# Combining expert results: second row added by an accumulating transfer instead of TensorE, residual rows and norm loaded into freed weight slots

## The chip, the cores and the metric

One Trainium2 chip (trn2), one core. The metric is the device time of one execution in microseconds (us); where several runs are told, it is their median.

## The reference

The model is a block of two layers on 1040 rows (16 meta rows and 1024 tokens) of width 1024, all in float32. Each layer is a mixer, a layer norm, a mixture of experts and a second layer norm; layer 0's mixer is an S5 scan beside differential attention, layer 1's is an RG-LRU. Every row goes to two of 32 experts, and the diff concerns what happens to their results:

```python
for i in range(DEPTH):
    ...
    h = _layer_norm(ALPHA * h + mix, *norms[i][0]).astype(dt)
    h = _layer_norm(ALPHA * h + _hier_moe(h, *moes[i]), *norms[i][1]).astype(dt)
return h[:, N_META:]

def _layer_norm(z, g, b):
    mu = jnp.mean(zf, -1, keepdims=True)
    var = jnp.mean(jnp.square(zf - mu), -1, keepdims=True)
    return (zf - mu) * lax.rsqrt(var + LN_EPS) * g + b

def _hier_moe(...):      # each row: the sum of two expert results, each times its gate
    ...
    y = jnp.zeros((T + 1, d), F32).at[slot_tok].add(yb.astype(F32) * slot_gate[:, None])
```

## The kernel before

The kernel runs in phases, one behind the other, each a block with one program per engine and its own semaphores. At the end of a phase `end_phase` clears them and all engines meet at a barrier (L2465, L2466). A phase therefore ends only when the last engine's program has ended, SyncE's included.

`experts_and_combine` (L1707 and on) is the phase of the experts, once for each layer. SyncE streams the 96 weight matrices of the layer (gate, up and down of 32 experts, 2 MB each) through a ring of ten slots, `E.ring`, in the order `W.units`; a slot is loaded again once the product that used it has been made. TensorE works through the groups of rows; the last four groups are single experts with many rows, and the very last a pair of small ones ("twins"). GpSimd gathers the input rows and scatters each result row, times its gate, into `K.y_dram` in HBM: the first expert's result of token t into row t, the second's into row T + t. When all scatters have landed it raises `rows_done`.

Then comes `Combining` (L2118 and on), in the same phase, over tiles of 128 rows: nine tiles in layer 0 (the first of 16 rows), eight in layer 1, which leaves the meta rows out.

- SyncE (`sync`, L2142): for each tile two loads from `y_dram` into `self.y` (L2149) and one of the residual rows from `h1_dram` into `K.H` (L2150), in four buffers, the norm's gain and bias (L1027, from `norm.load`) behind the second tile. Then for each tile a store of the finished rows (L2156). In layer 0 the weights (L2261 to L2264) and parameters (L2269, L2271) for the first blocks of the next stage are issued between the stores, behind the fifth. At the end it waits until all stores have landed.
- TensorE (`tensor`): `y_sum` (L2206) adds the two results of a tile into PSUM with an identity matrix. In layer 0 `turn` (L2215) transposes the finished rows for the next stage, three tiles behind.
- VectorE (`vector`, and `Norm.vector`): z = ALPHA * H + sum in two halves (L2187; tile 0 in two steps of full width from SBUF, L2182 and L2183), statistics (L1034, L1035), variance + eps (L1036), (z - mean) * gain (L1041), the reciprocal of the deviation (L1045). For the last tile it also multiplies and adds the bias (L1050).
- ScalarE (`scalar`): root of the variance (L1056), z times the reciprocal (L1060), and in layer 0 the copy of the transposed tile j - 2 behind the work on tile j (L2232). Its program order is fixed, so the root for tile j + 1 stands behind the copy of tile j - 2.
- GpSimd (`gpsimd`): adds the bias (L1068) for all tiles but the last.

In layer 0 the phase `rglru_and_project` follows; its first matmul is L2315. It projects `K.hT`, the transposed rows in SBUF; the rows stored in `h2_dram` are read again only as its last stage's residual.

Of the kernel before, what the change touches and what calls it, by code (L numbers as in the profile page):

```python
# [16 lines left out]
D = 1024  # L17
# [1308 lines left out]
X_BUFFERS = 3  # L1326

# [379 lines left out]
def experts_and_combine(nc, K, A, layer):  # L1707
# [30 lines left out]
    with ExitStack() as ctx:  # L1738
# [10 lines left out]
        def _(sp):  # L1749
            for u in range(HEAD_UNITS, 3 * NE):  # L1750
                r, kind = W.units[u]
                e = rank_register(sp, K, r)
                if u == HEAD_UNITS:
                    sp.wait_ge(gathered[0], 16)
                if u >= UNITS:
                    r_was, kind_was = W.units[u - UNITS]
                    i = W.last[r_was]
                    if kind_was == GATE:
                        sp.wait_ge(g_ready, i + 1)
                    elif kind_was == UP:  # L1760
                        sp.wait_ge(u_ready, i + 1)
                    elif by_dve[i]:
                        sp.wait_ge(yv_ready, dves[i + 1])
                    else:
                        sp.wait_ge(ya_ready, acts[i + 1])
                load_unit(sp, E, u, kind, e, E.loaded[u % UNITS])
            sp.wait_ge(ya_ready, acts[N])
# [350 lines left out]
class Combining:  # L2118
# [3 lines left out]
    BUFFERS = 4  # L2122

    def __init__(self, nc, K, A, layer, rows_done, ps, pt):
# [6 lines left out]
        self.y = [[at(f"{L}_y{k}{i}", [D]) for i in range(self.BUFFERS)] for k in range(2)]  # L2131
        self.norm = Norm(nc, K, L + "_ln2", at, self.first)
        assert self.last_layer or at.at <= K.lru.wz_at
# [3 lines left out]
        self.y_summed, self.z_done, self.order, self.turned, self.hT_ready, self.stored = map(sem, (  # L2137
            "y_summed", "z_done", "order", "turned", "hT_ready", "stored"))
        self.ps, self.pt = ps, pt

    def sync(self, sp):
# [397 lines left out]
```

## Time and profile before

| | us |
|---|---|
| median of 3 runs | 2360.32 |
| lowest and highest of them | 2356.91, 2366.04 |
| the profiled execution | 2361.56 |
| its span, first to last instruction | 2359.4 |
| granted TensorE clock, mean over the span | 0.961 of full |

| engine | busy, share of the span |
|---|---|
| TensorE, matmuls | 93% |
| VectorE | 33% |
| ScalarE | 21% |
| GpSimd | 13% |

The profile is of one execution. The engines' totals cover the whole span; the two combining stages take about 1184 to 1241 us and 2304 to 2359 us of it, under 5%. They are read with windows (busy time of each engine in a stretch) and with the timeline (single instructions in order of time, each with the idle time before it and what ended it). In the rows PE is TensorE's matmuls, PEld its weight loads, DVE VectorE, ACT ScalarE, POOL GpSimd and SPq SyncE's queue of DMA issues.

### The profile page before, as it was taken

The page shows a single profiled execution, that of the slowest core. Times are in us where ns is not written, and L with a number is a line of the kernel's source. Part 1 is how long each engine was busy: PE and PEld are TensorE (multiplying, and loading weights), DVE is VectorE, ACT ScalarE, POOL GpSimd, SP SyncE. Part 2 cuts the span into 40 slices and gives each one's busy share as a digit, 9 for nine tenths or more (in the row PEclk, how much of TensorE's full clock was granted, in tenths as well). Part 3 has the DMA queues.
Part 4 walks back from the last instruction along what each step waited for, and adds up shares of the span by engine and source line. Part 5 has one row for each costly group of instructions (what it writes and reads, how often), then busy time and mean ns, then how long its engine had stood idle before and what let it go on. Part 6 is the DMA issues. An engine that isn't in the chain of part 4 may idle for free. (4 is left out here: it accounts for less than half of the span.)

```text
span 2359.4 us, 33583 instructions
## 1 busy us (share of the span) xinstructions
PE 2193.0 (93%) x13491; PEld 1245.3 (53%) x13491; DVE 767.2 (33%) x1608; ACT 486.2 (21%) x904; POOL 309.0 (13%) x263
## 2 busy tenths in 40 slices
PE   8999999999689999999968999999968999999994
PEld 5778656655454455455434555555545455545541
DVE  7652236643611111111173344443251111111116
ACT  2222246611010001000033544431101000000001
POOL 7252000011011111111030000001101111111102
PEclk9999999999789999999988999999968999999998
DMA  4110001112399999899884111111139999989987
GB/s 159 38 37 1 21 1 72 32 46 71 152 393 419 420 419 418 332 407 409 357 299 163 40 40 27 33 39 46 62 152 380 413 419 419 419 348 391 414 368 306
DMA packets 148199, 529.81 MB, mean 225 GB/s; under 512 B 43874, under 2 KB 66946, under 8 KB 131664
## 3 DMA queue, kind: packets, MB, share of 16 engines
q1 hardware_dynamic: 134608, 493.84, 53.2%
q0 software_dynamic: 13312, 33.84, 3.8%
q8 instruction: 107, 1.75, 0.3%
q14 instruction: 44, 0.36, 0.0%
q10 hardware_dynamic: 128, 0.02, 0.0%
HBM read 499.99 MB, written 39.98 MB: 229 GB/s over the span
## 5 line engine op out<-in xcount | busy, mean ns | idle before, releaser
L1857 PE MATMUL l_main_pgu<-l_w_ring,l_ex_xT 128*64 128x256 f32 (+1 forms) x4992 | 474.1, 385 | 12.7 <-DMA l_w_ring<-in_l_moe_w_gate 9.8
L1857 PEld LDWEIGHTS l_main_pgu<-l_w_ring,l_ex_xT 128*64 128x64 f32 (+1 forms) x4992 | 285.6, 129 | 190.4 <-issue 40.9
L1903 PE MATMUL l_main_py<-l_w_ring,l_ex_hT 128*64 128x512 f32 (+1 forms) x1248 | 231.9, 594 | 1.9 <-DVE l_ex_hT L1974 1.9
L1854 PE MATMUL l_main_pgu<-l_w_ring,l_ex_xT 128*128 128x512 f32 x384 | 170.1, 596 | 3.3 <-DMA l_w_ring<-in_l_moe_w_gate 3.3
L1970 DVE TENSOR_TENSOR l_ex_hid<-l_ex_sil,l_main_pgu 128x256 f32<-128x256 f32 (+1 forms) x76 | 35.2, 464 | 377.0 <-PE l_main_pgu L1857 279.8
L1974 DVE COPY l_ex_hT<-l_main_ph 128x256 f32<-128x256 f32 (+1 forms) x76 | 35.5, 467 | 365.9 <-PE l_main_ph L1878 365.9
L2315 PE MATMUL lru_pr<-h2T,lru_wz 128*128 128x352 f32 (+1 forms) x480 | 144.4, 461 | 10.3 <-ACTq L2370 10.3
L2333 PE MATMUL lru_pg<-h2T,lru_wz 128*128 128x512 f32 x320 | 148.7, 592 | 0.0
L1903 PEld LDWEIGHTS l_main_py<-l_w_ring,l_ex_hT 128*64 128x64 f32 (+1 forms) x1248 | 69.1, 127 | 132.1 <-issue 124.8
L1946 ACT ACTIVATE l_ex_sil<-l_main_pgu 128x256 f32<-128x256 f32 (+1 forms) x76 | 31.8, 418 | 468.9 <-PE l_main_pgu L1857 374.7
L2315 PEld LDWEIGHTS lru_pr<-h2T,lru_wz 128*128 128x128 f32 x480 | 92.6, 193 | 63.1 <-ACTq L2370 10.7
L1854 PEld LDWEIGHTS l_main_pgu<-l_w_ring,l_ex_xT 128*128 128x128 f32 x384 | 71.2, 190 | 92.6 <-issue 87.0
L1798 POOL DMA_INDIRECT expert_rows<-l_ex_yb,half_row x64 | 64.4, 1006 | 414.5 <-issue 225.6
L308 PE MATMUL s_pa<-hT,w_in 128*128 128x260 f32 x512 | 114.7, 383 | 0.0
L1068 POOL TENSOR_TENSOR H<-H,l_ln_bias 128x1024 f32<-128x1024 f32 (+1 forms) x30 | 70.5, 2349 | 334.4 <-ACT H L1060 334.4
L1160 PE MATMUL lru_pr<-w_out,y1T 128*128 128x512 f32 x240 | 106.9, 602 | 0.0
L308 PEld LDWEIGHTS s_pa<-hT,w_in 128*128 128x128 f32 x512 | 96.9, 190 | 16.4 <-issue 1.7
L2333 PEld LDWEIGHTS lru_pg<-h2T,lru_wz 128*128 128x128 f32 x320 | 60.8, 190 | 57.1 <-issue 43.0
L1932 ACT COPY l_ex_xT<-l_main_px 128x512 f32<-128x512 f32 (+1 forms) x52 | 27.1, 521 | 295.8 <-PE l_main_px L1826 295.8
L2206 PE MATMUL l_main_pgu<-l_y,ident 128*128 128x512 f32 x88 | 45.2, 652 | 40.8 <-DMA H<-h_rows 40.5
L1784 POOL DMA_INDIRECT l_ex_xb<-h_rows,x_idx x36 | 37.5, 1041 | 343.9 <-PE l_main_px L1826 241.7
L1041 DVE SCALAR_TENSOR_TENSOR H<-H,l_ln_mean_var,l_ln_gain 128x1024 f32<-128x1024 f32 (+1 forms) x34 | 50.3, 1478 | 94.5 <-PE lru_pg L1185 46.2
(465 smaller groups left out, 2728.0 us busy)
## 6 DMA issues: line engine op xcount, KB each, us to landing
l_w_ring<-in_l_moe_w_gate SPq DMA_DIRECT2D x64, 2048.0 KB, 27.0
l_w_ring<-in_l_moe_w_up SPq DMA_DIRECT2D x64, 2048.0 KB, 27.9
l_w_ring<-in_l_moe_w_down SPq DMA_DIRECT2D x64, 2048.0 KB, 33.4
l_y<-expert_rows SPq DMA_DIRECT2D x32, 512.0 KB, 8.2
h_rows<-H SPq DMA_DIRECT2D x24, 512.0 KB, 5.3
lru_wz<-in_l_w_in SPq DMA_DIRECT2D x20, 512.0 KB, 4.9
w_in<-in_l_w_in SPq DMA_DIRECT2D x4, 2048.0 KB, 8.9
H<-h_rows SPq DMA_DIRECT2D x16, 512.0 KB, 9.9
```

The source lines that it names most:

```text
L308: last = pe.matmul(pa[n % 2][:, 0:STEPS], w[:, k, P * (f % HEADS):P * (f % HEADS) + P], hT[:, k, j, :], start=k == 0, stop=k == KD - 1)
L1041: dve.scalar_tensor_tensor(out=z, in0=z, scalar=self.mv[0:m, 0:1], in1=self.gain[0:m, :], op0=ALU.subtract, op1=ALU.mult).then_inc(self.ga ...
L1068: pool.tensor_tensor(z, z, self.bias[0:m, :], ALU.add).then_inc(self.h_ready, 1)
L1160: last = pe.matmul(po[j % 2][h][0:m, :], self.slices[k][:, t0:t0 + m], self.w_out[:, k, 512 * h:512 * h + 512], start=k == 0, stop=k == ns ...
L1784: pool.indirect_dma_start(xb[xn % 2][0:m, :], None, K.h1_dram, bass.IndirectOffsetOnAxis(ap=index, axis=0), bounds_check=T - 1, oob_is_err ...
L1798: pool.indirect_dma_start(y_halves, bass.IndirectOffsetOnAxis(ap=K.half_row[:, it.column:it.column + 1], axis=0), yb[i % 2][:, 0:512], Non ...
L1854: last = pe.matmul(out[:], x[:, k, :], w[0][:, k, :], start=k == 0, stop=k == KD - 1)
L1857: last = pe.matmul(out[HALF * h + o:HALF * h + o + m, 0:256], x[:, k, it.at + o:it.at + o + m], w[n][:, k, 256 * h:256 * h + 256], start=k ...
L1903: last = pe.matmul(py[b][HALF * h + o:HALF * h + o + m, :], hT[:, c % 2, HALF * (c // 2) + o:HALF * (c // 2) + o + m], ws[n][:, c, 512 * h ...
L2206: last = pe.matmul(self.ps[j % 2][h][0:m, :], K.ident[0:m, 0:m], self.y[k][j % B][0:m, 512 * h:512 * h + 512], start=k == 0, stop=k == 1)
L2315: last = pe.matmul(pr[j][:, 0:c], wz[par][:, k, 0, :], K.hT[:, k, o:o + c], start=k == 0, stop=k == KD - 1)
L2333: last = pe.matmul(pgt[j][:, 0:c], wz[par][:, k, 1, :], K.hT[:, k, N_META + o:N_META + o + c], start=k == 0, stop=k == KD - 1)
```

## The change

The combining of a tile takes one load by SyncE (the first expert's row) into one of nine buffers, and an accumulating transfer issued by GpSimd, which adds the second expert's row to it in SBUF. VectorE waits for this transfer and makes z in one step of full width, with both operands in SBUF. TensorE's `y_sum` is gone. GpSimd issues the accumulating transfers of all tiles, each behind a wait for that tile's load, before its first bias addition. The residual rows of all tiles are loaded ahead into `self.rows`, which lies in ring slots 6 to 8, and the norm's gain and bias into slot 9, each once the last product that used these slots is made; in layer 0 the next stage's parameters are loaded behind the norm. The next stage's weights are issued behind the loads of y, before the first store. In layer 0 SyncE no longer waits for the stores at the end of the phase, but in the next stage, before its projection.

```diff
         @block.sync
         def _(sp):
+            def unit_used(unit):
+                r, kind = W.units[unit]
+                i = W.last[r]
+                ...
             for u in range(HEAD_UNITS, 3 * NE):
                 ...
                 load_unit(sp, E, u, kind, e, E.loaded[u % UNITS])
+            for unit in range(3 * NE):
+                if unit + UNITS >= 3 * NE and unit % UNITS in ROW_UNITS:
+                    unit_used(unit)
+            combine.load_rows(sp)
+            for unit in range(3 * NE):
+                if unit + UNITS >= 3 * NE and unit % UNITS == NORM_UNIT:
+                    unit_used(unit)
+            combine.load_norm(sp)
             sp.wait_ge(ya_ready, acts[N])
             sp.wait_ge(yv_ready, dves[N])
             over.sync(sp)
@@ class Combining
-    BUFFERS = 4
+    BUFFERS = 9
...
+    def load_rows(self, sp):
+        for i in range(self.first, NT):
+            t0, m = TILES[i]
+            sp.dma_start(self.rows[0:m, i, :], self.K.h1_dram[t0:t0 + m, :]).then_inc(self.h1_loaded, 16)
+
+    def load_norm(self, sp):
+        self.norm.load(sp, self.A[self.L + "_ln2_g"], self.A[self.L + "_ln2_b"])
+        if not self.last_layer:
+            self.K.lru.load_parameters(sp)
...
             if j >= B:
-                sp.wait_ge(self.z_done, 2 * (j - B + 1))
-            for k in range(2):
-                sp.dma_start(self.y[k][j % B][0:m, :], K.y_dram[k * T + t0:k * T + t0 + m, :]).then_inc(self.loaded[j % B], 16)
-            sp.dma_start(K.H[0:m, self.first + j, :], K.h1_dram[t0:t0 + m, :]).then_inc(self.loaded[j % B], 16)
+                sp.wait_ge(self.z_done, j - B + 1)
+            sp.dma_start(self.y[j % B][0:m, :], K.y_dram[t0:t0 + m, :]).then_inc(self.loaded[j % B], 16)
...
-        for j in range(B):
+        for j in range(min(B, self.n)):
             load(j)
-            if j == 1:
-                norm.load(sp, self.A[self.L + "_ln2_g"], self.A[self.L + "_ln2_b"])
         for j in range(self.n):
             if j + B < self.n:
                 load(j + B)
+            if j == 0 and not self.last_layer:
+                K.lru.load_weights(sp, 0, 0)
+                K.lru.load_weights(sp, 1, 1)
             store(j)
-            if j == self.n - B - 1 and not self.last_layer:
-                K.lru.load_weights(sp, 0, 0)
-                K.lru.load_parameters(sp)
-                K.lru.load_weights(sp, 1, 1)
-        sp.wait_ge(self.stored, 16 * self.n)
+        if self.last_layer:
+            sp.wait_ge(self.stored, 16 * self.n)

     def vector(self, dve):
+        dve.wait_ge(self.h1_loaded, 16 * n)
         for j in range(n):
             ...
-            for h in range(2 if j else 0):
-                c = slice(512 * h, 512 * h + 512)
-                dve.wait_ge(self.y_summed, 2 * j + h - 1)
-                dve.scalar_tensor_tensor(out=z[:, c], in0=z[:, c], scalar=ALPHA, in1=self.ps[j % 2][h][0:m, :], op0=ALU.mult, op1=ALU.add).then_inc(self.z_done, 1)
-            dve.wait_ge(self.z_done, 2 * j + 2)
+            dve.wait_ge(self.added[j % self.BUFFERS], 16 * (j // self.BUFFERS + 1))
+            dve.scalar_tensor_tensor(out=K.H[0:m, i, :], in0=self.rows[0:m, i, :], scalar=ALPHA, in1=self.y[j % self.BUFFERS][0:m, :],
+                                     op0=ALU.mult, op1=ALU.add).then_inc(self.z_done, 1)
+            dve.wait_ge(self.z_done, j + 1)
             norm.vector(dve, do, i)

     def gpsimd(self, pool):
+        def add(j):
+            t0, m = TILES[self.first + j]
+            pool.wait_ge(self.loaded[j % B], 16 * (j // B + 1))
+            pool.dma_start(self.y[j % B][0:m, :], K.y_dram[T + t0:T + t0 + m, :], accum_op=ALU.add).then_inc(self.added[j % B], 16)
+
+        for j in range(n):
+            add(j)
         for i in range(self.first, NT - 1):
             self.norm.gpsimd(pool, i)

     def tensor(self, pe):
-        def y_sum(j):
-            ...
-        for j in range(n + 3):
-            if 0 < j < n:
-                y_sum(j)
-            if j >= 3 and not self.last_layer:
-                turn(j - 3)
+        for j in range(0 if self.last_layer else n):
+            turn(j)
@@ rglru_and_project, sync
             sp.wait_ge(gate_ready, NG * NB)
+            sp.wait_ge(*K.h2_stored)
             project.sync(sp)
```

The rest of the diff places the buffers.

## Rows read from the trace of the kernel before

**Rows 1.** The page's part 1, TensorE: busy us, share of the span, instructions.

```profile
PE 2193.0 (93%) x13491; PEld 1245.3 (53%) x13491; DVE 767.2 (33%) x1608; ACT 486.2 (21%) x904; POOL 309.0 (13%) x263
```

**Rows 2.** Windows, layer 0: busy us by engine, TensorE clock, DMA share, GB/s.

```profile
1165.00:1175.00 10.00, 9.04 (x42) 3.69 (x38) 1.50 (x3) 1.97 (x2) 0.78 (x1) 1.00 0.51 203
1175.00:1183.00 8.00, 2.30 (x24) 0.49 (x16) 0.75 (x1) 0.00 (x0) 1.18 (x2) 0.85 0.19 74
...
1210.00:1220.00 10.00, 10.00 (x38) 5.37 (x37) 9.76 (x19) 4.63 (x8) 5.05 (x3) 1.00 1.02 412
...
1240.00:1250.00 10.00, 0.00 (x0) 0.00 (x0) 0.15 (x3) 0.99 (x3) 0.00 (x0) 0.50 0.80 284
```

**Rows 3.** Timeline, starts of both stages: start us, us, engine, line, what, [idle before].

```profile
1183.71 1.03 SPq L2149 DMA_DIRECT2D l_y<-expert_rows  x2
...
1195.57 1.27 DVE L1041 SCALAR_TENSOR_TENSOR H<-H,l_ln_mean_var,l_ln_gain 16x1024 f32<-16x1024 f32 x1 [4.07 <-DMA l_ln_bias<-in_l_ln_b]
...
2304.14 1.62 SPq L2149 DMA_DIRECT2D l_y<-expert_rows  x2
...
2312.00 1.22 DVE L2182 SCALAR_TENSOR_TENSOR H<-H,l_y 128x1024 f32<-128x1024 f32 x1 [12.36 <-DMA H<-h_rows]
...
2319.48 1.29 DVE L1041 SCALAR_TENSOR_TENSOR H<-H,l_ln_mean_var,l_ln_gain 128x1024 f32<-128x1024 f32 x1 [3.16 <-DMA l_ln_bias<-in_l_ln_b]
```

**Rows 4.** Timeline, one tile of the steady loop, layer 0.

```profile
1207.22 0.15 DVE L1045 RECIPROCAL l_ln_rec_dev<-l_ln_dev 128x1 f32<-128x1 f32 x1
...
1208.69 2.36 POOL L1068 TENSOR_TENSOR H<-H,l_ln_bias 128x1024 f32<-128x1024 f32 x1 [2.48 <-ACT H L1060]
...
1210.29 1.85 DVE L1041 SCALAR_TENSOR_TENSOR H<-H,l_ln_mean_var,l_ln_gain 128x1024 f32<-128x1024 f32 x1
...
1212.06 0.15 DVE L1045 RECIPROCAL l_ln_rec_dev<-l_ln_dev 128x1 f32<-128x1 f32 x1
```

**Rows 5.** Timeline, VectorE beside GpSimd, elsewhere and in layer 1.

```profile
503.47 2.34 POOL L1068 TENSOR_TENSOR H<-H,l_ln_bias 128x1024 f32<-128x1024 f32 x1 [14.89 <-ACT H L1060]
503.56 2.26 DVE L1491 TENSOR_TENSOR rc_work<-rc_work,rc_steps 128x1 f32<-128x1 f32 x1
...
2322.24 2.34 POOL L1068 TENSOR_TENSOR H<-H,l_ln_bias 128x1024 f32<-128x1024 f32 x1 [20.66 <-ACT H L1060]
2322.32 0.69 DVE L2187 SCALAR_TENSOR_TENSOR H<-H,l_main_ph 128x512 f32<-128x512 f32 x1 [0.84 <-PE l_main_ph L2206]
```

**Rows 6.** Timeline, ends of the experts and of both stages.

```profile
1168.88 3.60 PE L1895 MATMUL l_main_py<-l_w_ring,l_ex_hT 128*128 128x512 f32 x8
...
1236.47 1.28 DVE L1050 SCALAR_TENSOR_TENSOR H<-H,l_ln_rec_dev,l_ln_bias 128x1024 f32<-128x1024 f32 x1
...
1239.63 3.46 SPq L2156 DMA_DIRECT2D h_rows<-H  x4
...
1239.81 1.07 ACT L2232 COPY h2T<-l_main_px 128x512 f32<-128x512 f32 x2 [1.47 <-PE l_main_px L2215]
...
1250.08 10.14 PE L2315 MATMUL lru_pr<-h2T,lru_wz 128*128 128x352 f32 x24 [10.31 <-ACTq L2370]
...
2355.09 1.28 DVE L1050 SCALAR_TENSOR_TENSOR H<-H,l_ln_rec_dev,l_ln_bias 128x1024 f32<-128x1024 f32 x1
```

**Rows 7.** Waits of SyncE in 1150 to 1260: total us, times, longest.

```profile
SPq L1738 <- DMA h_rows<-H: 5.2, 1, 5.2
```

**Rows 8.** Timeline of SyncE's issues, layer 0.

```profile
1221.59 3.18 SPq L2262 DMA_DIRECT2D lru_wz<-in_l_w_in  x1
...
1228.68 4.08 SPq L2269 DMA_DIRECT2D lru_prm<-in_l_conv_w  x4
```

**Rows 9.** DMA issues of large-expert scatters: whole run, then last one: us to landing.

```profile
expert_rows<-l_ex_yb,big_row POOLq DMA_INDIRECT x12, 7.5
...
expert_rows<-l_ex_yb,big_row POOLq DMA_INDIRECT x1, 3.2
```

**Rows 10.** Timeline, the last scatter of layer 0.

```profile
1179.06 0.98 POOL L1798 DMA_INDIRECT expert_rows<-l_ex_yb,half_row  x1 [3.87 <-DVE l_ex_yb L1982]
```

More of the change, by code:

```diff
@@ L1326 @@
 X_BUFFERS = 3
+ROW_UNITS, NORM_UNIT = (6, 7, 8), 9
 class Item:
@@ L1749, in _ @@
         def _(sp):
+            def unit_used(unit):
+                r, kind = W.units[unit]
+                i = W.last[r]
+                if kind == GATE:
+                    sp.wait_ge(g_ready, i + 1)
+                elif kind == UP:
+                    sp.wait_ge(u_ready, i + 1)
+                elif by_dve[i]:
+                    sp.wait_ge(yv_ready, dves[i + 1])
+                else:
+                    sp.wait_ge(ya_ready, acts[i + 1])
             for u in range(HEAD_UNITS, 3 * NE):
@@ L2130, in __init__ @@
         K.hT = None if self.last_layer else at("h2T", [KD, T])
-        self.y = [[at(f"{L}_y{k}{i}", [D]) for i in range(self.BUFFERS)] for k in range(2)]
+        self.y = [at(f"{L}_y{i}", [D]) for i in range(self.BUFFERS)]
+        assert self.last_layer or at.at <= K.lru.loaded_at
+        unit_at = lambda unit: (K.base + 31) // 32 * 32 + unit * KD * F * 4
+        at = Place(nc, unit_at(NORM_UNIT) - NT * D * 4)
+        assert at.at >= unit_at(ROW_UNITS[0]) and (self.last_layer or at.at >= K.lru.loaded_end)
+        self.rows = at(f"{L}_h1_rows", [NT, D])
         self.norm = Norm(nc, K, L + "_ln2", at, self.first)
-        assert self.last_layer or at.at <= K.lru.wz_at
+        assert at.at <= unit_at(NORM_UNIT + 1)
         sem = lambda n: K.sem(f"{L}_cb_{n}")
@@ L2136, in __init__ @@
         self.loaded = [sem(f"loaded{i}") for i in range(self.BUFFERS)]
-        self.y_summed, self.z_done, self.order, self.turned, self.hT_ready, self.stored = map(sem, (
-            "y_summed", "z_done", "order", "turned", "hT_ready", "stored"))
+        self.added = [sem(f"added{i}") for i in range(self.BUFFERS)]
+        self.z_done, self.order, self.turned, self.hT_ready, self.h1_loaded = map(sem, (
+            "z_done", "order", "turned", "hT_ready", "h1_loaded"))
+        self.stored = nc.alloc_semaphore(f"{L}_cb_stored")
         self.ps, self.pt = ps, pt
+        if not self.last_layer:
+            K.h2_stored = self.stored, 16 * self.n
+    def load_rows(self, sp):
[4 more added lines that the diff above has]
+        self.norm.load(sp, self.A[self.L + "_ln2_g"], self.A[self.L + "_ln2_b"])
+        if not self.last_layer:
+            self.K.lru.load_parameters(sp)
     def sync(self, sp):
@@ L2196, in tensor @@
         K, n, first, B = self.K, self.n, self.first, self.BUFFERS
-        def y_sum(j):
-            m = TILES[first + j][1]
-            pe.wait_ge(self.loaded[j % B], 48 * (j // B + 1))
-            if j >= 2:
-                pe.wait_ge(self.z_done, 2 * (j - 1))
-            for h in range(2):
-                for k in range(2):
-                    last = pe.matmul(self.ps[j % 2][h][0:m, :], K.ident[0:m, 0:m], self.y[k][j % B][0:m, 512 * h:512 * h + 512], start=k == 0, stop=k == 1)
-                last.then_inc(self.y_summed, 1)
         def turn(j):
@@ L2249, in __init__ @@
         assert K.route_constants.free <= at.at and K.route_constants.start >= self.wz_at + 2 * 2 * P * 4
-        self.prm, self.pc = at("lru_prm", [9, NB]), at("lru_pc", [9])
-        self.m = [at(f"lru_m{i}", [NB]) for i in range(4)]
+        self.prm = at("lru_prm", [9, NB])
+        self.loaded_end = at.at
         self.gg, self.ra, self.ii, self.a, self.t = (at("lru_" + n, [T]) for n in ("gg", "r", "i", "a", "t"))
+        self.pc, self.m = at("lru_pc", [9]), [at(f"lru_m{i}", [NB]) for i in range(4)]
         assert at.at <= K.w_out1_at
```

18 lines of the change are left out of this document (3 added, 15 removed).

## The prediction

> **What bounds the kernel now.** I read the engines' totals first [rows 1]: TensorE is busy 93% of the span. That is an average over stages, and says nothing of the two short stages that the diff touches, the combining behind each layer's experts. So I read windows inside them [rows 2]. In 1210 to 1220 us TensorE is full, but so are VectorE (9.76 of 10 us) and the DMA engines (share 1.02, 412 GB/s), and GpSimd is half busy. Which of them sets the pace has to be read from one tile in order of time [rows 4]: reciprocal 1207.22, ScalarE's multiplication behind it, GpSimd's bias addition 1208.69 to 1211.05, VectorE's L1041 from 1210.29 to 1212.14, next reciprocal 1212.06. The period is 4.84 us. L1041 takes 1.85 us here and 1.29 us where GpSimd is idle [rows 3], and ends 1.09 us behind GpSimd's end: it is held until GpSimd lets go. The same is seen far away, where a VectorE addition of one column takes 2.26 us and ends with GpSimd's 2.34 us operation [rows 5], while the combining step L2187, which has one operand in PSUM, takes its 0.69 us beside GpSimd undisturbed [rows 5]. So the loop is reciprocal, ScalarE, GpSimd, L1041, reciprocal. TensorE's sums stand outside it.
>
> Ahead of the loop is a start: in layer 0 the first loads go out at 1183.71 and L1041 of tile 0, last to wait for the norm's bias, runs at 1195.57; in layer 1 it is 2304.14 and 2319.48 [rows 3]. Behind it is an end: in layer 0 VectorE finishes at 1237.75 and the last transposed copy ends at 1240.88, but the next stage's first matmul is at 1250.08 [rows 6], because SyncE issued the last four stores only at 1239.63 to 1243.09 and then waited 5.2 us for them [rows 6, 7], with 1.8 us to pass the barrier. In layer 1 VectorE finishes at 2356.37 [rows 6], which with the last store's landing is the end.
>
> **The change part by part.**
> *TensorE's sums go* (two halves of 0.69 us on VectorE per tile become one step of 1.22 us from SBUF [rows 3, 5]). VectorE saves 0.15 us a tile, but that only makes L1041 arrive earlier at a lock that opens when GpSimd ends: in the steady loop it is worth 0. The new step has both operands in SBUF. With GpSimd in step it runs from reciprocal + 0.11 to + 1.35 us, just ahead of GpSimd's start at + 1.47, so there it costs nothing; this cover is gone when GpSimd lags (below). Without GpSimd a tile would take 4.84 - 0.56 - 0.15 = 4.1 us.
>
> *Layer 0's store wait goes.* After the last VectorE step (E) come 3.1 us of transpose and copy and 1.8 us of barrier: the next stage starts at E + 4.9 instead of E + 12.3. That is -7.4 us at an unchanged E. LRU weights are issued earlier, so nothing in that stage becomes late; the store wait at its end is long over. TensorE's granted clock in 1240 to 1250 us, ahead of that stage, is 0.50, its lower level (1.2 GHz), already [rows 2], so the missing sums make that start no colder.
>
> *Rows and norm are loaded early.* Once the last large expert's gate and up matmuls are done, before its down product at 1168.88 [rows 6], SyncE puts 4.3 MB of rows on its queue behind the last weights, so they delay no weights. The norm's 1 MB goes out at about 1172.5. In layer 1 rows and norm (5.3 MB, 12.8 us at 412 GB/s, in a stretch that as in layer 0 has about 203 and 74 GB/s in use [rows 2]) are in by about 2305; the last scatter shares with them, which I price at 0.7 us of later start. The first L1041 no longer waits for the bias. In layer 0 the eight parameter loads ride along, and SyncE stands behind them. Four of them took 4.08 us to issue in the trace, and an issue of a strided weight took 3.18 us where the queue was full [rows 8]. Rows and norm fill the queue until about 1183 to 1185, so seven of the eight parameter loads are issued behind that, about 1 us each, and the first y load comes at about 1189 instead of 1183.71. Bounds: 1184.5 (no back-pressure) and 1192.
>
> *The additions in the transfer.* Each y tile is loaded (1.28 us of all DMA engines for 512 KB at 412 GB/s, the first about 4.5 us after its issue, as three of them and their waits take 7.9 us from 2304.14 to 2312.00 [rows 3]), then GpSimd issues the accumulating transfer (0.98 us for an issue [rows 10]). The trace has no accumulating transfer. Nearest rows: a plain 512 KB scatter from GpSimd lands in 3.2 us with the engines free and in a median of 7.5 us beside the weight stream [rows 9]. So its occupancy lies between 1.28 us (as a plain load) and 4.3 us (the difference of the two). It reads the rows in HBM and the tile in SBUF and writes the tile; I take one load plus one store, 2.56 us. The Trainium skill (Collectives: The Full Stack, on why ReduceScatter is half of AllGather) says that an add in the DMA engines reads two sources and so runs at half the copy rate. By that rule the price is 2.56 us and the time 2368.5 us; by the lower bound, the copy rate, it would be 2358 us. No row here shows which.
>
> *GpSimd's order is the new wait.* All additions are issued ahead of the first bias addition, so GpSimd's norm work for tile 0 queues behind the wait for the last tile's load. Loads and additions are on two queues that share the engines, so the loads slow to 1.28 + 2.56 = 3.84 us a tile once additions flow.
> Layer 1: first loads 2304.8, tile 0 lands 2309.3, its addition is landed about 2316 (first-landing, issue and some 5 us beside the loads, between the two scatters), and L1041 is 3 us behind it, as behind the reciprocal in the loop (3.07 [rows 4]): 2319, 0.5 us before now; loads of tiles 0 to 2 arrive 1.3 us apart, the others 3.84 us: the last at about 2332, GpSimd's first bias addition at P = 2333.5, where it now stands at 2322.24 [rows 5]. VectorE meanwhile runs at 4.1 us a tile and GpSimd has four tiles of backlog. While it catches up the lock alternates: 2.35 (GpSimd) + 1.1 (VectorE) = 3.45 us for each of GpSimd's seven tiles, then 1.3 us of last step: 2333.5 + 24.2 + 1.3 = 2359 to 2360 against 2356.37. **+3.2 us.**
> Layer 0: y loads from 1189, tile 1 lands 1193.5, tile 2 1194.8, tile 8 six steps of 3.84 later, 1217.8, P = 1219. Here ScalarE's order binds too: the copy of transposed tile 0 stands ahead of the root for tile 3, so reciprocal 3 waits for GpSimd's tile 0 (2.4), its transposes, copies and the root (1.7, a 16-row tile; the last tile's transposes and copies take 3.1): P + 4.1 = 1223.1. In the trace reciprocal 3 is at 1212.06 and VectorE ends 25.7 us later [rows 4, 6]; with about 1.2 us of lock waits for the backlog of two: E = 1250, the next stage starts at 1254.9 against 1250.08. **+4.8 us**, the 7.4 us of the store wait already in it.
>
> Sum: +8.0 us. The profiled execution took 2361.56 us (span 2359.4 and 2.2 us around it), 1.2 us above the median of 2360.32, so the forecast is **2368.5 us** (+0.35%).
>
> **The rivals.**
> *An addition costs what a load costs* (1.28 us). Loads come 2.56 us apart: in layer 1 P = 2327 and VectorE ends at about 2356.7 (+0.3); in layer 0 P = 1211.5, E = 1242.5, the stage starts at 1247.4 (-2.7). Sum -2.4, **2358 us**. For it: stores and loads together already fill the engines at the same 412 GB/s.
> *GpSimd is not late.* The loads, all issued before the first addition, pass ahead and the parameters do not hold SyncE: P = 1200 to 1202 and 2320 to 2322. Then the old loop runs from an earlier start: layer 0 ends at about 1235.3, stage start 1240.2 (-9.9); layer 1 saves 2.7. Sum -12.6, **2348 us**. Against it: the 7.5 us of the scatters beside weights show that queues share.
> *Slow additions*, the one that ends clearly slower: at 4.3 us each the loads are 5.6 us apart, P = 2342 and 1229.5, ends 2367.5 (+11) and a stage start of 1265.4 (+15). Sum +26, **2387 us**. Above 3 us an addition the change costs more than 0.5%.
>
> **How the numbers follow.** Forecast 0.42 (its own range 2362 to 2376), cheap additions 0.20, GpSimd in time 0.15, slow additions 0.18, others 0.05. The range reaches to the third and fourth case: 2348 to 2388. A measurement tells about 0.5% (11.8 us) from no change; below 2348.5 lies most of the third case and a little of others (0.15), above 2372 all of the fourth and a quarter of the forecast's spread (0.30), leaving 0.55.
>
> **What would show it.** GpSimd's first bias addition in each combining stage (forecast 1219 and 2333.5): right or wrong, this decides. SyncE's first y load in layer 0 at about 1189 with long issues of parameter loads before it. Median landing of the additions and the spacing of the y landings (3.8 us). L1041 at 1.85 us or more and the new combining step above 1.3 us while GpSimd catches up, 1.25 where it doesn't. No wait for stores before the LRU stage, whose first matmul is 4.9 us behind VectorE's last step. Wrong if the loads pass ahead of the additions, if GpSimd's operations do not hold the new step, or if an addition is far from 2.56 us.

## The result and the profile after

| | before | after |
|---|---|---|
| median of 5 runs, us | 2360.32 | 2379.14 |
| lowest and highest, us | 2356.91, 2366.04 | 2375.07, 2384.88 |
| span of the profiled execution, us | 2359.4 | 2377.3 |
| mean granted TensorE clock | 0.961 | 0.943 |

The ratio is 1.0072, 95% interval 1.0056 to 1.0087: 0.7% slower, which is 17 us by the ratio; the two medians lie 18.8 us apart. The forecast was 2368.5 us in a range of 2348 to 2388: the time lies inside it, on the side that was forecast, but the change costs twice the 8 us of the sum.

The windows show the stretch in which loads and additions share the DMA engines (the columns of [rows 2]):

```profile
1210.00:1220.00 10.00, 0.00 (x0) 0.00 (x0) 8.97 (x17) 2.70 (x4) 2.58 (x3) 0.50 1.06 275
...
2330.00:2340.00 10.00, 0.00 (x0) 0.00 (x0) 8.35 (x15) 1.56 (x4) 2.53 (x3) 0.50 1.06 261
```

Against the same window of before (1210 to 1220 us in [rows 2]), TensorE has gone from full to empty and its granted clock from 1.00 to 0.50. The DMA engines are as full as before (1.06 against 1.02), but move 275 GB/s and not 412. Being busy they now do less; the experiment with plain copies below shows that this is the accumulating transfer.

The timeline of after, both stages (the columns of [rows 3]; L2180 is the load of the first expert's rows, L2220 the accumulating transfer, L2209 VectorE's new combining step, L2289 the first four parameter loads, L1811 the last scatter, L2336 the next stage's first matmul):

```profile
1178.25 15.59 SPq L2289 DMA_DIRECT2D lru_prm<-in_l_conv_w  x4
...
1184.23 0.98 POOL L1811 DMA_INDIRECT expert_rows<-l_ex_yb,half_row  x1 [4.16 <-DVE l_ex_yb L1995]
...
1199.57 4.25 SPq L2180 DMA_DIRECT2D l_y<-expert_rows  x9
...
1214.30 0.86 POOL L2220 DMA_DIRECT2D l_y<-expert_rows  x1 [2.91 <-DMA l_y<-expert_rows]
...
1218.15 0.86 POOL L2220 DMA_DIRECT2D l_y<-expert_rows  x1 [2.99 <-DMA l_y<-expert_rows]
...
1221.92 0.86 POOL L2220 DMA_DIRECT2D l_y<-expert_rows  x1 [2.90 <-DMA l_y<-expert_rows]
...
1222.20 8.33 DVE L2209 SCALAR_TENSOR_TENSOR H<-l_h_rows,l_y 128x1024 f32<-128x1024 f32 x1
1222.48 6.96 POOL L1068 TENSOR_TENSOR H<-H,l_ln_bias 16x1024 f32<-16x1024 f32 x3
...
1233.39 0.16 DVE L1045 RECIPROCAL l_ln_rec_dev<-l_ln_dev 128x1 f32<-128x1 f32 x1
...
1257.76 1.28 DVE L1050 SCALAR_TENSOR_TENSOR H<-H,l_ln_rec_dev,l_ln_bias 128x1024 f32<-128x1024 f32 x1
...
1264.27 11.08 PE L2336 MATMUL lru_pr<-h2T,lru_wz 128*128 128x352 f32 x31 [3.28 <-ACTq L2391]
...
2309.36 0.99 POOL L1811 DMA_INDIRECT expert_rows<-l_ex_yb,half_row  x1 [3.87 <-DVE l_ex_yb L1995]
...
2316.98 4.64 SPq L2180 DMA_DIRECT2D l_y<-expert_rows  x8
...
2321.51 0.96 POOL L2220 DMA_DIRECT2D l_y<-expert_rows  x1 [11.17 <-DMA l_y<-expert_rows]
...
2331.45 1.23 DVE L2209 SCALAR_TENSOR_TENSOR H<-l_h_rows,l_y 128x1024 f32<-128x1024 f32 x1 [23.04 <-DMA l_y<-expert_rows]
...
2341.45 0.85 POOL L2220 DMA_DIRECT2D l_y<-expert_rows  x1 [2.98 <-DMA l_y<-expert_rows]
...
2342.02 4.95 POOL L1068 TENSOR_TENSOR H<-H,l_ln_bias 128x1024 f32<-128x1024 f32 x2
...
2342.75 5.31 DVE L1041 SCALAR_TENSOR_TENSOR H<-H,l_ln_mean_var,l_ln_gain 128x1024 f32<-128x1024 f32 x1
...
2350.99 1.89 DVE L1041 SCALAR_TENSOR_TENSOR H<-H,l_ln_mean_var,l_ln_gain 128x1024 f32<-128x1024 f32 x1
...
2372.33 1.28 DVE L1050 SCALAR_TENSOR_TENSOR H<-H,l_ln_rec_dev,l_ln_bias 128x1024 f32<-128x1024 f32 x1
```

Read it from the last scatter of each layer, because that point moves by itself: over the single executions of the kernels below it lies anywhere from 1173.9 to 1185.1 us in layer 0, with no order in what was changed. In us behind that scatter (before: [rows 10] and, in layer 1, a scatter at 2300.59):

| | layer 0 before | forecast | after | layer 1 before | forecast | after |
|---|---|---|---|---|---|---|
| first load of y | 4.65 | 9.9 | 15.34 | 3.55 | 4.2 | 7.62 |
| GpSimd's first bias addition, P | 19.3 | 39.9 | 38.25 | 21.65 | 32.9 | 32.66 |
| VectorE's last step ends, E | 58.7 | 70.9 | 74.81 | 55.8 | 59.0 | 64.25 |
| next stage's first matmul | 71.0 | 75.8 | 80.04 | | | |

Layer 0 costs 80.04 - 71.02 = 9.0 us (forecast 4.8), layer 1 64.25 - 55.78 = 8.5 us (forecast 3.2): together 17.5 of the spans' difference of 17.9. That they agree so closely is partly luck: the last scatter of layer 0 comes 5.2 us later in after, and from the next stage's start to the last scatter of layer 1 it takes 5.4 us less (1045.1 against 1050.5). That stretch takes 1042.3 to 1051.2 us in the profiled executions of the kernels below, again with no order in what was changed.

What SyncE waited for ahead of layer 1's loads, from after's waits behind 2270 us (line waited at and releaser: us, times, longest):

```profile
SPq L2180 <- POOLq L1827: 8.3, 1, 8.3
```

L1827 is GpSimd's signal that all scatters have landed. The window around the last scatter (2309.36) shows the DMA engines full, with rows and norm still on their way:

```profile
2305.00:2310.00 5.00, 2.59 (x27) 0.52 (x16) 0.75 (x1) 0.00 (x0) 1.13 (x2) 1.00 1.03 412
```

The landing of after's transfers over the whole run (the columns of [rows 9]):

```profile
l_h_rows<-h_rows SPq DMA_DIRECT2D x16, 512.0 KB, 15.7
...
l_y<-expert_rows SPq DMA_DIRECT2D x16, 512.0 KB, 8.2
l_y<-expert_rows POOLq DMA_DIRECT2D x16, 512.0 KB, 13.2
```

In the median, an addition lands 13.2 us after its issue, a load 8.2 us; the residual rows, queued behind the last weights, take 15.7 us.

### The profile page after: what moved, and what is told of

The parts are those of the page before. It is cut to its first block and busy times, and to the rows that moved or that the text cites. A ratio compares the mean times of both kernels' runs of the same rounds, so it can differ in the third digit from the quotient of the medians.

```text
span 2377.3 us, 33315 instructions
## 1 busy us (share of the span) xinstructions
PE 2138.7 (90%) x13371; PEld 1225.6 (52%) x13371; DVE 773.7 (33%) x1591; ACT 485.8 (20%) x904; POOL 323.0 (14%) x280
## 5 line engine op out<-in xcount | busy, mean ns | idle before, releaser
L2336 PE MATMUL lru_pr<-h2T,lru_wz 128*128 128x352 f32 (+1 forms) x480 | 143.2, 459 | 3.3 <-ACTq L2391 3.3
L1811 POOL DMA_INDIRECT expert_rows<-l_ex_yb,half_row x64 | 64.3, 1004 | 415.5 <-issue 225.8
L2336 PEld LDWEIGHTS lru_pr<-h2T,lru_wz 128*128 128x128 f32 x480 | 92.1, 192 | 55.4 <-issue 5.5
L1041 DVE SCALAR_TENSOR_TENSOR H<-H,l_ln_mean_var,l_ln_gain 128x1024 f32<-128x1024 f32 (+1 forms) x34 | 53.7, 1578 | 87.1 <-PE lru_pg L1185 46.4
## 6 DMA issues: line engine op xcount, KB each, us to landing
l_w_ring<-in_l_moe_w_down SPq DMA_DIRECT2D x64, 2048.0 KB, 31.6
l_h_rows<-h_rows SPq DMA_DIRECT2D x16, 512.0 KB, 15.7
```

The lines of the kernel that those rows point to most:

```text
L1041: dve.scalar_tensor_tensor(out=z, in0=z, scalar=self.mv[0:m, 0:1], in1=self.gain[0:m, :], op0=ALU.subtract, op1=ALU.mult).then_inc(self.ga ...
L1811: pool.indirect_dma_start(y_halves, bass.IndirectOffsetOnAxis(ap=K.half_row[:, it.column:it.column + 1], axis=0), yb[i % 2][:, 0:512], Non ...
L2336: last = pe.matmul(pr[j][:, 0:c], wz[par][:, k, 0, :], K.hT[:, k, o:o + c], start=k == 0, stop=k == KD - 1)
```

## The experiments

The theory to begin with: the cost is the late start of the loads plus GpSimd's bias additions queued behind the last addition, during which VectorE is held. The rivals: the additions fill the DMA engines whatever GpSimd's order is; the early rows do the harm; or the store wait removed is worth less than 7.4 us. Each ratio is against the kernel before on the same chip.

**The parameters behind the loads (5 rounds).** The kernel after, with this edit:

```diff
     def load_norm(self, sp):
         self.norm.load(...)
-        if not self.last_layer:
-            self.K.lru.load_parameters(sp)
...
                 K.lru.load_weights(sp, 1, 1)
+                K.lru.load_parameters(sp)
             store(j)
```

> The changed kernel with one thing undone: the eight parameter loads of the next stage are issued behind the y loads and the next stage's weights, not behind the norm. Theory (late start): in layer 0 SyncE is held by these loads, so its first y load comes 15.3 us behind GpSimd's last scatter, 7.6 us in layer 1 where there are none. It should now come at about 7.6 us in layer 0 too, and the LRU stage start 7 to 8 us earlier: 2379 - 7.5 = 2371.5 us. Rival (the accumulating transfer is the cost): the start moves but the ends of both stages hardly do, 2377 to 2380 us.

Measured: 2370.36 us, ratio 1.0041 [1.0024, 1.0058]. Its timeline:

```profile
1189.62 5.06 SPq L2178 DMA_DIRECT2D l_y<-expert_rows  x9
...
1216.04 6.24 DVE L1041 SCALAR_TENSOR_TENSOR H<-H,l_ln_mean_var,l_ln_gain 128x1024 f32<-128x1024 f32 x1
```

The last scatter is at 1181.86: the first load comes 7.8 us behind it, where after has 15.3, and the next stage starts at +71.4 instead of +80.0. So the eight parameter loads, four of which took 15.59 us to issue, held SyncE, and the whole stage with it. The loads are still 3 us later than before's +4.65, and the last scatter lands 6.8 us after its issue, where it takes 3.9 us in the kernel with the later store wait alone, which has no early rows. VectorE is still held for 6.24 us in one L1041.

**GpSimd issues four additions, then alternates (5 rounds).** The kernel after, with this edit:

```diff
-        for j in range(n):
+        for j in range(4):
             add(j)
-        for i in range(self.first, NT - 1):
+        for j in range(4, n):
+            self.norm.gpsimd(pool, self.first + j - 4)
+            add(j)
+        for i in range(self.first + n - 4, NT - 1):
             self.norm.gpsimd(pool, i)
```

> The changed kernel, but GpSimd issues the first four additions and then one bias addition and one further addition in turn. Theory (GpSimd's order): there is no backlog any more, so no VectorE step of 5 to 8 us; from the first L1041 every tile takes 4.83 us. Layer 0: first L1041 27.4 us behind the last scatter, end of VectorE at 27.4 + 8 x 4.83 + 3.4 = 69.5 instead of 74.8 us; layer 1: 25.0 + 7 x 4.83 + 3.4 = 62.2 instead of 64.3. Sum -7.4 us, 2371.7 us. Rival (the transfers' own cost): GpSimd would wait for loads in between as before, VectorE gets no tile earlier, under 2 us change.

Measured: 2374.3 us, ratio 1.0046 [1.0031, 1.0061]. E is at +69.5 and +62.5, as expected, with the loads as late as in after (+15.2 and +8.4). GpSimd's timeline in layer 0:

```profile
1212.89 3.18 POOL L1068 TENSOR_TENSOR H<-H,l_ln_bias 16x1024 f32<-16x1024 f32 x1 [6.16 <-ACT H L1060]
1216.03 0.58 POOL L2220 DMA_DIRECT2D l_y<-expert_rows  x1
1218.55 2.34 POOL L1068 TENSOR_TENSOR H<-H,l_ln_bias 128x1024 f32<-128x1024 f32 x1 [1.94 <-ACT H L1060]
```

The first bias addition now waits for ScalarE, not for the last load, and the longest L1041 is 1.90 us in layer 0 and 1.97 in layer 1, where it was 5.31; L2209, which was held for 8.33 us, takes 1.23 us or less in every tile. GpSimd's order alone is worth 5.3 and 1.8 us at E. The rival that the additions fill the DMA engines in any order is false for these 7 us.

**Both edits together (5 rounds).**

> The changed kernel with both repairs: parameter loads behind the y loads, and additions issued between the bias additions. If the two causes are separate, they add up: layer 0's first L1041 19.4 us behind the last scatter as with the first repair alone, then 8 x 4.83 + 3.4, so VectorE ends at 61.4 and the LRU stage starts at 66.8 us (before: 71.0); layer 1 ends at 62.5 us (before: 55.8). Sum +2.5 us against the kernel before: 2363 us. If one cause hides the other it stays at 2370 us.

Measured: 2364.88 us, ratio 1.0001 [0.9991, 1.0011]. The next stage starts at +68.3 (before: +71.0), layer 1 ends at +62.3 (before: +55.8). With both repairs the change is worth nothing: the store wait that it removes pays for what the rest still costs. The two places are worth the whole 0.7% (by the ratios 0.31% and 0.26% when each is mended alone).

**A plain copy for the addition (5 rounds).** The same transfer without `accum_op`: it writes over the first expert's rows, and so leaves the first expert's result out of the sum.

> The changed kernel with GpSimd's transfers as plain copies of the same bytes to the same place (the first expert's result is left out of the sum). It measures the price of accumulating. Theory (an accumulating tile takes 2.56 us of all DMA engines, a plain one 1.28): landings of y are 2.5 us apart instead of 3.8, GpSimd's first bias addition 5 to 7 us earlier in each stage, and as VectorE has fewer tiles ready by then the ends move 3 to 5 us each: 2371 us. Rival (accumulating is the whole loss): 2362 us or less.

Measured: 2374.16 us, ratio 1.0042 [1.0027, 1.0057]. Its timeline:

```profile
1214.17 8.01 POOL L1068 TENSOR_TENSOR H<-H,l_ln_bias 16x1024 f32<-16x1024 f32 x3
...
1214.76 2.92 DVE L1041 SCALAR_TENSOR_TENSOR H<-H,l_ln_mean_var,l_ln_gain 128x1024 f32<-128x1024 f32 x1
...
1217.71 5.56 DVE L2209 SCALAR_TENSOR_TENSOR H<-l_h_rows,l_y 128x1024 f32<-128x1024 f32 x1
...
2332.88 0.53 POOL L2220 DMA_DIRECT2D l_y<-expert_rows  x1 [2.03 <-DMA l_y<-expert_rows]
2335.43 0.53 POOL L2220 DMA_DIRECT2D l_y<-expert_rows  x1 [2.02 <-DMA l_y<-expert_rows]
...
2336.62 3.26 DVE L2209 SCALAR_TENSOR_TENSOR H<-l_h_rows,l_y 128x1024 f32<-128x1024 f32 x1
```

A window of the same kernel in layer 1 (the columns of [rows 2]):

```profile
2325.00:2335.00 10.00, 0.00 (x0) 0.00 (x0) 6.61 (x10) 1.35 (x2) 2.11 (x4) 0.50 1.02 412
```

And the landing of its copies (the columns of [rows 9]):

```profile
l_y<-expert_rows POOLq DMA_DIRECT2D x16, 512.0 KB, 8.7
```

GpSimd waits for each load, so the distance of its issues is the distance of the loads. With copies they are 2.55 us apart (a load and a copy, 1.28 us each) at 412 GB/s; with additions 3.77 to 3.85. The addition therefore takes 3.8 - 1.28 = 2.5 us of the DMA engines, twice a copy, as the sum had it. The Trainium skill (Collectives: The Full Stack, on why ReduceScatter is half of AllGather) has an add read two sources and run at half the rate: the trace agrees on the rate, at 2.5 us for 512 KB against 1.28; no row shows the second read itself. The last issue comes 3.4 us (layer 0) and 4.9 us (layer 1) earlier than in after, but VectorE's ends only 2.4 and 3.7 us, where 3 to 5 us each were expected. By the ratios the kernel gains 0.3%. GpSimd's backlog is still there: three and two waiting tiles, as in after.

**Residual rows and norm late (3 rounds).** The first edit above, and the rows loaded tile by tile beside y:

```diff
-            combine.load_rows(sp)
...
-            combine.load_norm(sp)
...
             sp.dma_start(self.y[j % B][0:m, :], ...).then_inc(self.loaded[j % B], 16)
+            sp.dma_start(self.rows[0:m, self.first + j, :], ...).then_inc(self.loaded[j % B], 16)
+            if j == 1:
+                self.load_norm(sp)
...
-            pool.wait_ge(self.loaded[j % B], 16 * (j // B + 1))
+            pool.wait_ge(self.loaded[j % B], 32 * (j // B + 1))
```

> The changed kernel with parameters behind (as a1), and the rows and norm not loaded early: each tile's rows go out behind its y load, the norm behind the second tile. Theory: the first y load comes at 4 to 5 us behind the last scatter instead of 7.6, since nothing shares the engines with the scatter, but loads and additions now take 5.1 us of the DMA engines a tile, so the last load, on which GpSimd's first bias addition waits, comes 12 to 15 us later and the ends of both stages 7 to 10 us: 2387 us. Rival (the early loads, which slow the last scatter, are a loss of 3.5 us in each layer and nothing else): 2364 us.

Measured: 2398.68 us, ratio 1.0151 [1.0134, 1.0169]. The direction was right, the size too small: the last addition is issued at +48.7 in layer 0, where the first experiment had +31.6. Its profiled execution took 2384.52 us, 14 us under the median; the times from the scatters on, which are read here, give 28 us more than in the first experiment, as the medians do. Its timeline in layer 1:

```profile
2354.85 11.82 POOL L1068 TENSOR_TENSOR H<-H,l_ln_bias 128x1024 f32<-128x1024 f32 x5
...
2355.13 12.64 DVE L1041 SCALAR_TENSOR_TENSOR H<-H,l_ln_mean_var,l_ln_gain 128x1024 f32<-128x1024 f32 x1
```

Five bias additions back to back, and VectorE shut out for all of them. So the early rows and norm don't harm the change as a whole: without them it costs 1.5% where the first experiment costs 0.4%. The first loads do come earlier without them, at +5.2 and +5.8 instead of +7.8 and +7.4, but in layer 1 not as early as before's +3.55.

**The later store wait alone (5 rounds).** The kernel before, with:

```diff
-        sp.wait_ge(self.stored, 16 * self.n)
+        if self.last_layer:
+            sp.wait_ge(self.stored, 16 * self.n)
...
             sp.wait_ge(gate_ready, NG * NB)
+            sp.wait_ge(*K.h2_stored)
             project.sync(sp)
```

> The kernel before with one part of the change alone: layer 0's stores are awaited in the next stage, not at the end of the phase. Theory: the LRU stage starts 4.9 us behind VectorE's last step instead of 12.3 us, 7.4 us earlier, and that carries to the end: 2353 us. Rival (another wait takes its place, the weights that SyncE issues at 1236 to 1240 us or the stores beside the first weights): under 3 us, 2358 us.

Measured: 2357.42 us, ratio 0.9970 [0.9957, 0.9983], that is -7.1 us by the ratio (-4.0 to -10.2) and -5.1 between the medians, against the -7.4 of the sum. Its timeline:

```profile
1242.70 1.28 DVE L1050 SCALAR_TENSOR_TENSOR H<-H,l_ln_rec_dev,l_ln_bias 128x1024 f32<-128x1024 f32 x1
...
1245.82 3.51 SPq L2159 DMA_DIRECT2D h_rows<-H  x4
...
1251.19 5.05 PE L2320 MATMUL lru_pr<-h2T,lru_wz 128*128 128x352 f32 x10 [5.18 <-ACTq L2375]
```

The wait is gone, but the last four stores are still issued after VectorE's end (1243.98), and the next stage starts 7.2 us behind it, not 4.9. The traces of one execution each give -4.9 us from the last scatter to the next stage's start: the mechanism is there, but by the trace 2.3 us of the 7.4 are not got, because SyncE is late with its stores.

**The change without accumulating transfers (5 rounds).** TensorE's sums and the four buffers of before; rows and norm early, the store wait later; weights and parameters issued between the stores:

```diff
             store(j)
+            if not self.last_layer:
+                if j == 1:
+                    K.lru.load_weights(sp, 0, 0)
+                if j == 3:
+                    K.lru.load_parameters(sp)
+                if j == 5:
+                    K.lru.load_weights(sp, 1, 1)
```

> The change without the accumulating transfers: TensorE adds as before, rows and norm are loaded early, stores are awaited later, and the next stage's weights and parameters are issued between the stores. Theory: the start still comes at 7.6 us, but the first L1041 does not wait for the norm: about 14 us in layer 0 (before 16.5) and 17 in layer 1 (18.9); the loop runs at 4.83 us as before; the LRU stage starts 5 us behind VectorE's end. Layer 0: 61.5 instead of 71.0 us, layer 1: 54 instead of 55.8. Sum -11 us, 2349 us. Rival (the late scatter eats what the early rows bring): only the store wait is left, 2353 us.

Measured: 2362.39 us, ratio 0.9992 [0.9980, 1.0004]. A miss by 13 us. Its timeline:

```profile
1223.83 6.72 SPq L2304 DMA_DIRECT2D lru_prm<-in_l_conv_w  x4
...
1233.89 1.32 SPq L2178 DMA_DIRECT2D l_y<-expert_rows  x2
...
1244.81 0.69 DVE L2218 SCALAR_TENSOR_TENSOR H<-l_h_rows,l_main_pgu 128x512 f32<-128x512 f32 x1 [5.73 <-PE l_main_pgu L2239]
```

I had put the parameters ahead of the last tile's loads, and they held SyncE for 10 us: the same mistake as in the change, at another place. The last tile's reciprocal comes 12.1 us behind the one before it, where the loop has 4.8, which is 7 us. Another 4.6 us of layer 0 are lost at the second tile, whose reciprocal comes 9.4 us behind the first; VectorE waits there for TensorE's sum, whose first half takes 3.78 us (as in the experiment with the early norm below). In layer 1, which has no parameters, the end is at +56.0, where before has +55.8, although the first L1041 runs 1.6 us earlier. The early rows bring nothing to the kernel with sums.

**The parameters issued by ScalarE (5 rounds).** The later store wait, and ScalarE, idle ahead of the stage, issues the eight parameter loads:

```diff
-                K.lru.load_parameters(sp)
...
     def scalar(self, act):
+        if not self.last_layer:
+            self.K.lru.load_parameters(act)
```

> The kernel before with the stores awaited later (as b1), and the eight parameter loads issued by ScalarE when its expert work is done, where it is idle for some 20 us and the DMA engines are nearly so. Theory: in b1 SyncE still issued parameters between the stores, so its last stores went out late and the LRU stage started 7.2 us behind VectorE's last step instead of about 5. Now 63.9 us behind the last scatter instead of 66.1 (before: 71.0), the rest as b1: 2 us under b1, ratio 0.996, about 2353 us. Rival (4-byte packets beside the last expert weights delay these): the last scatter comes later and the time is that of b1 or above.

Measured: 2355.69 us, ratio 0.9966 [0.9954, 0.9978]. Its timeline:

```profile
1171.67 3.30 ACTq L2274 DMA_DIRECT2D lru_prm<-in_l_conv_w  x4
...
1234.71 6.89 SPq L2159 DMA_DIRECT2D h_rows<-H  x4
```

The same four loads took 3.30 us on ScalarE here and 4.08 on SyncE before [rows 8], where they took 6.72 and 15.59 behind other transfers. The next stage starts 4.9 us behind VectorE's end, as the prediction had it for this wait. But VectorE's end comes 2.0 us later behind the last scatter than with the later wait alone (+60.9 against +58.9), so the next stage starts at +65.7 where it started at +66.1. What ScalarE's issues add to the later wait alone is not separable from its 0.9970.

**The norm early as well (5 rounds).** The kernel just told, with the norm's gain and bias loaded into ring slot 9 once it is free, as the change does.

> c1b with the norm's gain and bias loaded into ring slot 9 as in the change, but no rows. Theory: 1 MB less stands in the full queue at the start, and L1041 of tile 0 doesn't wait for the bias (4.1 and 3.2 us of idle before it): first L1041 at 13 to 14 us behind the last scatter instead of 16.5, and 16 instead of 18.9, both ends 2 to 2.5 us earlier: 2348 us. Rival (the early 1 MB slows the last scatter, and TensorE's sum of tile 1, held by its own loads, is next): the start moves by under 1 us and the time stays at that of c1b.

Measured: 2356.41 us, ratio 0.9974 [0.9964, 0.9985]. The first L1041 comes at +13.4 and +15.3 (+17.9 and +18.7 without the edit), but E is at +60.3 and +56.0, as without it (+60.9 and +56.1). The timeline says who takes the gain:

```profile
1188.06 1.26 DVE L1041 SCALAR_TENSOR_TENSOR H<-H,l_ln_mean_var,l_ln_gain 16x1024 f32<-16x1024 f32 x1
...
1189.53 3.78 PE L2214 MATMUL l_main_pgu<-l_y,ident 128*128 128x512 f32 x4 [16.59 <-DMA H<-h_rows]
...
1193.41 0.69 DVE L2195 SCALAR_TENSOR_TENSOR H<-H,l_main_pgu 128x512 f32<-128x512 f32 x1 [4.02 <-PE l_main_pgu L2214]
```

A window of it (the columns of [rows 2]):

```profile
1189.50:1193.30 3.80, 3.77 (x5) 1.71 (x6) 0.00 (x0) 1.14 (x1) 2.33 (x1) 0.50 1.02 409
```

VectorE is done with the first tile at 1189.39 and waits 4.0 us for the first half of the second tile's sum. Only 0.14 us of that are loads that haven't landed: TensorE starts at 1189.53 and needs 3.78 us for the half, at a granted clock of 0.50, the lower of its two levels (1.2 GHz). At 1.00 the same half takes 1.88 us (before, at 1205.09). In before this sum, also 3.78 us long, was hidden behind the wait for the bias: it began at 1192.56, and L1041 ran at 1195.57. The expectation's rival had the second tile's sum next in line and the time unchanged, and so it came; it was wrong only in that the first L1041 would hardly move.

**GpSimd kept out of step (5 rounds).** The kernel before; GpSimd's bias addition of tile j waits for VectorE's L1041 of tile j + 1:

```diff
         pool.wait_ge(self.scaled, j + 1)
+        if self.name.endswith("ln2"):
+            pool.wait_ge(self.gained, j + 2)
```

> The kernel before with one wait added: GpSimd's bias addition of tile j waits until L1041 of tile j + 1 is done. If the loop is set by GpSimd holding L1041, L1041 takes 1.28 us in every tile and a tile 4.3 us instead of 4.83, less 2.3 us for the last tile, whose last step now waits for GpSimd: -1.6 us in layer 0, -1.0 in layer 1, 2357.5 us. If VectorE is held by the transfers instead (three loads and a store take 5.1 us of the DMA engines a tile), L1041 is short too but VectorE waits for loads, and the time stays or grows to 2363 us.

Measured: 2372.75 us, ratio 1.0031 [1.0018, 1.0044]. Its timeline:

```profile
2349.41 1.28 DVE L1041 SCALAR_TENSOR_TENSOR H<-H,l_ln_mean_var,l_ln_gain 128x1024 f32<-128x1024 f32 x1
...
2352.16 0.69 DVE L2189 SCALAR_TENSOR_TENSOR H<-H,l_main_ph 128x512 f32<-128x512 f32 x1 [0.75 <-PE l_main_ph L2208]
...
2358.42 1.28 DVE L1050 SCALAR_TENSOR_TENSOR H<-H,l_ln_rec_dev,l_ln_bias 128x1024 f32<-128x1024 f32 x1 [2.55 <-POOL H L1070]
```

L1041 takes 1.27 or 1.28 us in every tile of layer 1, where most took 1.83 or 1.84 (1.85 in layer 0 [rows 4]): the 0.57 us are the hold by GpSimd. In layer 0:

```profile
1223.14 3.70 PE L2208 MATMUL l_main_pgu<-l_y,ident 128*128 128x512 f32 x8 [2.40 <-DMA H<-h_rows]
...
1225.23 0.69 DVE L2189 SCALAR_TENSOR_TENSOR H<-H,l_main_pgu 128x512 f32<-128x512 f32 x1 [1.18 <-PE l_main_pgu L2208]
```

Three tiles in a row follow each other by 4.27 us, as expected; then VectorE waits for TensorE's sums, and these wait for the loads. Over the whole of layer 0's stage the reciprocals are 4.93 us apart on the mean, with the edit and without it, and the last step waits 2.55 us more for GpSimd. So the rival named in the expectation, three loads and a store for each tile, is the next bound, right behind the hold. The time is worse than either had it: E comes 3.3 and 2.0 us later, and by the ratio the kernel loses 7 us.

## Why the prediction was right in kind and short in size

**The bound was named rightly.** In after, once the backlog is gone, L1041 is at 1.89 us and the tiles follow each other by 4.82 us, with TensorE's sums gone and the DMA engines not full (share 0.71 in 2345 to 2360 us). Their removal bought nothing in the loop, as costed. In before the loads stand close behind as the next bound, as the last experiment shows; the prediction doesn't say so.

**The store wait: right.** The next stage starts 5.2 us behind E in after (forecast 4.9) instead of 12.3. Alone in the kernel before, the later wait is worth 7.1 us by the ratio, but 5.1 between the medians and 4.9 in the trace (forecast 7.4).

**The price of an addition: right.** 2.5 us, forecast 2.56, between bounds of 1.28 and 4.3. The rivals of cheap and of slow additions fall by this term alone.

**GpSimd's new wait: right in place and time.** P was forecast at +39.9 and +32.9 and came at +38.3 and +32.7. Two errors cancel in it. The loads started 5.4 and 3.4 us later than I had it. But only the last few stood 3.8 us apart (in layer 0 the last three issues, where I had counted six steps), since the first loads went through before additions flowed.

**The late start in layer 0: too small.** I had the first load at about 1189 with 1192 as the upper bound, 10 to 13 us behind the scatter; it was 15.3. The step that failed is "seven of the eight parameter loads are issued behind that, about 1 us each". Four of them took 15.59 us. The first experiment undoes it: 7.6 us at the first load and 8.7 us at the next stage's start. I had bounded an issue behind a full queue by [rows 8], issues of 3.18 and 4.08 us. In after the same two issues take 13.30 us (the strided weight, L2282, behind the loads of y) and 15.59 us (the four parameter loads).

**The last scatter in layer 1: too cheap.** Its landing beside rows and norm was priced at 0.7 us; the first load comes 7.6 us behind its issue and not 3.55, which is 4.1 us. The scatter lands in 7.0 us, with the DMA engines at a share of 1.03. [rows 9] had that price, 7.5 us beside the weight stream; the prediction added only 0.7 us to the case of free engines (3.2 us). With the rows late the first load still came at +5.75, so one execution gives 1.9 of the 4.1 us to rows and norm; the rest is open.

**The lock: the step that failed for the rest.** "While it catches up the lock alternates", I wrote, 3.45 us for each of GpSimd's tiles. It doesn't. In after GpSimd runs its three or two waiting tiles back to back, and one VectorE instruction waits through all of them: L2209 for 8.33 us instead of 1.23, L1041 for 5.31 instead of 1.28. The same stands in the first experiment (6.24) and in the late rows (five tiles, 12.64). Only with plain copies did VectorE get through behind the first waiting tile: in layer 0 with L1041 in 2.92 us, and L2209 then waited 5.56, and in layer 1 with L2209 in 3.26 us, while GpSimd's two tiles took 6.11 us instead of 4.95. What lets it in is open.

In layer 0 this gives all of the miss behind P. I had reciprocal 3 at P + 4.1, behind GpSimd's first tile alone, and 1.2 us of further lock waits; it is at 1233.39, P + 10.9. From there to E it takes 25.7 us, as before. That is 5.6 us, less the 1.7 by which P was early, plus 0.3 at the start of the next stage: 4.2, the whole difference between 9.0 and 4.8.

In layer 1 it is rather the count of waiting tiles. I had four at P. The first addition landed 9.9 us after its issue (2321.51 to 2331.45), where I had put some 5, so VectorE had finished only two tiles. A waiting tile costs GpSimd 2.35 us and a tile not yet begun 4.82, so from P to E it takes 24.4 us with five tiles waiting (the late rows) and 31.6 with two (after): (31.6 - 24.4)/3 = 2.4 us a tile. Two tiles fewer than forecast are 4.8 of the 5.3 us missed. With four waiting it would have been 31.6 - 2 x 2.4 = 26.8 us, near the 26.1 of the sum: there the wrong model of the lock gives nearly the right number.

**The clock.** The mean granted clock fell from 0.961 to 0.943: from 1200 to 1241 us, in layer 0's stage, it is 0.50 in after, where TensorE has only its transposes, and 0.93 in before, where it had the sums. The next stage's first matmuls were at 0.50 in before too, and its start shows no cost: its first 48 matmuls take 15.89 us in after and 17.03 in before (15.8 to 17.3 over all the kernels).

**What stays open.** Both repairs leave layer 1 6.5 us longer than before; the later first load (+5.0 us) carries most of it, and no run separates the rest. No version with accumulating transfers beat before. The fastest kernels here are before with the later store wait, with or without the parameters on ScalarE and the early norm: 0.9966, 0.9970 and 0.9974, with overlapping intervals.

## What to carry to other kernels

A change that moves work to an idle engine also moves what that engine has queued behind it: look which later work of GpSimd or SyncE waits for the new instruction, and let it alternate with the old work rather than run ahead of it. Many small strided loads can hold the engine that issues them for far longer than their bytes say (15.6 us for four of 5 KB here), so issue them where nothing urgent stands behind, or from an engine with nothing to do. And of a bundle of edits, run the one-line one alone: here the later store wait was worth 0.3% by itself, and the bundle around it made the kernel 0.7% slower.

## What the runs showed of the hardware that I had not expected

- GpSimd's waiting instructions kept a VectorE instruction out through the whole backlog: 8.33 us behind three tiles, 12.64 behind five. With plain copies alone one VectorE instruction got through in each layer. L2209's record begins at 1222.20, 0.28 us ahead of GpSimd's at 1222.48, and it still waited for 7 us. The Trainium skill (SBUF — State Buffer, "Who interferes with whom") says that a VectorE instruction with two SBUF inputs contends with a GpSimd instruction that reads SBUF, and, of VectorE's two-port modes, that whoever issues first gets the pair of ports that both share for its whole instruction. The 1.85 us of the loop, which end 1.09 us behind GpSimd's end, agree with a hold for a whole instruction; this row doesn't agree with the first to issue, as far as the records' starts show the order.
- Four parameter loads of 5 KB each took 3.30, 4.06, 6.72 and 15.59 us to issue, by what stood in the queues ahead of them: 15.6 us in each of the three kernels that issue them on SyncE behind rows and norm. They landed 9.7 us after issue in after, 3.6 in before (medians).
- A DMA engine share of 1.06 stood beside 261 to 275 GB/s with additions and 1.02 beside 412 with copies: the share alone doesn't say how much is moved.
- An accumulating transfer's issue took 0.83 to 0.96 us on GpSimd in after, the same transfer without addition 0.53 to 0.60.
- The same half of a sum took TensorE 3.78 us at a granted clock of 0.50 and 1.88 us at 1.00.
